# Forget-gate bias of the attention scores: from a DRAM round trip and a masked tile to a second matmul into the same bank

## The reference

```python
def forgetting_attention(q, k, v, logf):
    c = jnp.cumsum(logf, axis=-1)                       # (heads, 256)
    for i in range(S // Q_BLOCK):                       # two blocks of 128 queries
        q0, q1 = i * Q_BLOCK, (i + 1) * Q_BLOCK
        logits = einsum('bhqd,bhkd->bhqk', q[:, :, q0:q1], k[:, :, :q1]) * scale
        logits = logits + (c[:, :, q0:q1, None] - c[:, :, None, :q1])
        logits = jnp.where(causal, logits, -jnp.inf)
        p = jax.nn.softmax(logits, axis=-1)
        outs.append(einsum('bhqk,bhkd->bhqd', p, v[:, :, :q1]))
```

## Time and profile before

| | |
|---|---|
| time, median of 3 runs | 1739.52 us (1736.98 to 1743.05) |
| the profiled execution's own time | 1739.52 us |
| its span, first to last instruction | 1737.6 us |
| mean granted TensorE clock | 0.97 of full speed |
| TensorE busy | 1639.4 us (94%) |
| VectorE busy | 1104.8 us (64%) |
| ScalarE busy | 813.6 us (47%) |
| GpSimd busy | 112.6 us (6%) |

### The profile page before, as it was taken

The page is one execution under the profiler, slowest core; times in us unless marked ns, Lnnn a source line. Parts: engine busy times, 40 slices in busy tenths (PEclk is TensorE's granted clock), DMA queues, the critical chain, the costliest instruction groups (busy, mean ns, idle before and its releaser), DMA issues.

```text
span 1737.6 us, 29051 instructions
## 1 busy us (share of the span) xinstructions
PE 1639.4 (94%) x12246; PEld 1547.7 (89%) x12246; DVE 1104.8 (64%) x1382; ACT 813.6 (47%) x1064; POOL 112.6 (6%) x99
## 2 busy tenths in 40 slices
PE   7999899999999989999888999989999999899998
PEld 6999889998989889999878899978999999799997
DVE  5766768775676668777586566667766544265554
ACT  5454354444534444444586544445444443254442
POOL 1310000000140000000020000001111111000000
PEclk9999999999999999999998999999999999599999
DMA  8856356656676437665432366667765444035552
GB/s 273 274 199 206 110 202 221 232 194 223 217 257 236 141 118 246 215 230 203 157 114 94 114 222 236 241 230 233 252 207 182 146 158 134 25 121 189 182 188 97
DMA packets 232322, 326.62 MB, mean 188 GB/s; under 512 B 7704, under 2 KB 201728, under 8 KB 231680
## 3 DMA queue, kind: packets, MB, share of 16 engines
q1 hardware_dynamic: 222888, 316.16, 54.1%
q10 hardware_dynamic: 9304, 8.59, 1.6%
HBM read 315.28 MB, written 9.45 MB: 187 GB/s over the span
## 4 chain that ended last, share of the span: by engine, by line
PE 75%; issue 8%; DVE 8%; ACT 5%; DMA 2%; POOL 1%; SPq 0%; ACTq 0%; POOLq 0%; DVEq 0%
PE bank L472 23%; PE bank L473 22%; PE bank L474 22%; ACT whi L1019 2%; PE bank L513 2%; DVE wlo L1471 2%; DMA raw<-in_w_in 2%; PE bank L534 1%; POOL rstd L958 1%; PE bank L842 1%; PE bank L670 1%; PE bank L862 1%; PE bank L602 1%; DMA raw<-in_w_ffn_in 1%; PE bank L852 1%
## 5 line engine op out<-in xcount | busy, mean ns | idle before, releaser
L1471 DVE TENSOR_TENSOR wlo<-raw,whi 128x2048 fp32r<-128x2048 f32 (+1 forms) x241 | 548.3, 2277 | 296.6 <-ACT whi L1019 296.3
L1019 ACT ACTIVATE whi<-raw 128x2048 fp32r<-128x2048 f32 (+1 forms) x241 | 456.0, 1894 | 143.0 <-PE bank L474 108.9
L472 PE MATMUL bank<-hT_hi,whi 128*128 128x256 f32 x1728 | 496.9, 288 | 6.6 <-DVE wlo L1471 6.0
L473 PE MATMUL bank<-hT_lo,whi 128*128 128x256 f32 x1728 | 491.3, 284 | 0.0
L474 PE MATMUL bank<-hT_hi,wlo 128*128 128x256 f32 x1728 | 491.2, 284 | 0.0
L472 PEld LDWEIGHTS bank<-hT_hi,whi 128*128 128x128 f32 x1728 | 334.0, 193 | 13.9 <-DVE wlo L1471 6.8
L473 PEld LDWEIGHTS bank<-hT_lo,whi 128*128 128x128 f32 x1728 | 334.2, 193 | 1.2
L474 PEld LDWEIGHTS bank<-hT_hi,wlo 128*128 128x128 f32 x1728 | 333.9, 193 | 0.0
L472 PE MATMUL bank<-whi,hT_hi 128*128 128x256 f32 (+1 forms) x944 | 276.4, 293 | 13.6 <-DVE hT_lo L1534 6.6
L473 PE MATMUL bank<-wlo,hT_hi 128*128 128x256 f32 (+1 forms) x944 | 271.5, 288 | 0.0
L474 PE MATMUL bank<-whi,hT_lo 128*128 128x256 f32 (+1 forms) x944 | 271.3, 287 | 0.0
(11 more groups left out here) (272 smaller groups left out, 1615.3 us busy)
## 6 DMA issues: line engine op xcount, KB each, us to landing
raw<-in_mlp_w SPq DMA_DIRECT2D x64, 1024.0 KB, 5.5
ada_raw<-in_ada_w SPq DMA_DIRECT2D x96, 512.0 KB, 6.4
raw<-in_w_in SPq DMA_DIRECT2D x44, 1024.0 KB, 5.9
raw<-in_w_ffn_in SPq DMA_DIRECT2D x44, 1024.0 KB, 5.2
raw<-in_dil_w_in SPq DMA_DIRECT2D x36, 1024.0 KB, 5.1
raw<-in_w_ffn_out SPq DMA_DIRECT2D x22, 1024.0 KB, 5.0
raw<-in_w_o SPq DMA_DIRECT2D x8, 1024.0 KB, 5.1
bias_near<-near SPq DMA_DIRECT2D x2, 3072.0 KB, 10.3
```

The source lines that it names most:

```text
L472: pe.matmul(dst, lh, rh, start=start, stop=False)
L473: pe.matmul(dst, lh, rl, start=False, stop=False)
L1019: act.activation(view(whi[c % SPL], c), view(raw[c % RAW], c), ACT.Copy).then_inc(s_hi, 1)
L1471: dve.tensor_tensor(view(wlo[c % SPL], c), view(raw[c % RAW], c), view(whi[c % SPL], c).bitcast(F32), ALU.subtract).then_inc(s_lo, 1)
```

## The change

In a score unit each of the two matmuls is followed by a second one into the same columns that accumulates (`start=False`): its stationary operand is column i of the first 8 rows of the identity matrix, spread over 128 columns, and its moving operand is `ncum`, 8 rows. So it adds row i of `ncum` to each of the 128 queries. TensorE waits once for `ncum` ahead of the first unit of a layer. VectorE then reads the mask alone in place of `lbias`; the mask is widened to 384 columns (triangle, zeros, triangle) and is the same for all heads. The store to DRAM, the two spreading DMAs, the waits of SP, and the mask's additions on GpSimd go. `sqh`, `qn` and `mt` get buffers of their own. In layer 0 the angles now stand ahead of `ncum` on VectorE.

```diff
-    c["causal"] = tri
+    c["causal"] = np.concatenate([tri, np.zeros((P, P), np.float32), tri], axis=1)
...
-            lbias = sb("lbias", [P, H1, 3 * P], at=ph)
-            flat = lbias[:, :, :].rearrange("p h k -> p (h k)")
-            sqh = [flat[:, 512 * i:512 * i + 512] for i in range(2)]
-            qn, mt = ([flat[:, a + 512 * i:a + 512 * i + 512].rearrange("p (t n) -> p t n", t=TT) for i in range(2)]
-                      for a in (1024, 2048))
+            sqh = [sb(f"sqh{i}", [P, 512], at=ph) for i in range(2)]
+            qn = [sb(f"qn{i}", [P, TT, 256], at=ph) for i in range(2)]
...
+            mt = [sb(f"mt{i}", [P, 2, S], at=ph) for i in range(2)]
...
+                pe.wait_ge(s_cum, l + 1)
                 g = 0
                 for i in range(H1 + 3):
...
                         for q0, q1, c0 in ((0, P, 0), (P, S, P)):
-                            m = pe.matmul(bk[:, c0:c0 + q1], qT1[r0:r0 + 64, t, q0:q1], kT1[r0:r0 + 64, t, 0:q1],
-                                          start=True, stop=True)
+                            pe.matmul(bk[:, c0:c0 + q1], qT1[r0:r0 + 64, t, q0:q1], kT1[r0:r0 + 64, t, 0:q1],
+                                      start=True, stop=False)
+                            m = pe.matmul(bk[:, c0:c0 + q1], ident[0:H1, i:i + 1].broadcast_to([H1, P]),
+                                          ncum[:, 0:q1], start=False, stop=True)
                         end(m, ("S", u))
...
-                if name[0] == "G" and name[2] == 0:
-                    l = name[1]
-                    sp.wait_ge(s_cum, l + 1)
-                    sp.dma_start(sums_dram[l], ncum[:, :]).then_inc(s_sumsout, 16)
-                    sp.wait_ge(s_sumsout, 16 * (l + 1))
-                    emptied(sp, ("qkT", 4 * l + 3))
-                    for n, k0 in ((1, 0), (2, P)):
-                        sp.dma_start(lbias[:, :, k0:k0 + n * P], sums_dram[l, :, 0:n * P].unsqueeze(0).broadcast_to([P, H1, n * P]))\
-                          .then_inc(s_sumsin, 16)
...
-                pool.wait_ge(s_causal, 16)
-                pool.wait_ge(s_sumsin, 32 * (l + 1))
-                for h in range(H1):
-                    masked = lbias[:, h, :].rearrange("p (s k) -> p s k", k=P)[:, 0:3:2, :]
-                    pool.tensor_tensor(masked, masked, causal[:, :].unsqueeze(1).broadcast_to([P, 2, P]), ALU.add).then_inc(s_lbias, 1)
...
+                if l == 0:
+                    angles()
                 dve.wait_ge(s_zt, l + 1)
                 link(dve.tensor_tensor(mf[:, :], tf[:, :], mf[:, :], ALU.subtract))
                 dve.tensor_tensor_scan(ncum[:, :], mf[:, :], zero1[:, :].broadcast_to([H1, S]), 0.0, ALU.add, ALU.add)\
                    .then_inc(s_cum, 1)
-                if l == 0:
-                    angles()
...
+                dve.wait_ge(s_causal, 16)
...
-                        dve.wait_ge(s_lbias, u + 1)
...
-                            ins = dve.tensor_tensor_reduce(L1[u % 2][:, a:b], bk[:, a:b], lbias[:, i, a:b], 1.0, NEG,
+                            ins = dve.tensor_tensor_reduce(L1[u % 2][:, a:b], bk[:, a:b], causal[:, a:b], 1.0, NEG,
                                                            ALU.add, ALU.max, mx[:, u % 2, t:t + 1])
```

More of the change, by code:

```diff
@@ L105, in block_pair @@
         far_dram = nc.dram_tensor("bias_far", (TT, P, DH, P), F32, kind="Internal").ap()
-        sums_dram = nc.dram_tensor("forget_sums", (DEPTH, H1, S), F32, kind="Internal").ap()
         near_dram = nc.dram_tensor("bias_near", (TT, P, DH, NG * P), F32, kind="Internal").ap()
@@ L117, in block_pair @@
         ident = sb("ident", [P, P])
-        causal = sb("causal", [P, P])
+        causal = sb("causal", [P, 3 * P])
         invcount = sb("invcount", [P, 2, S])
@@ L241, in block_pair @@
         s_fw, s_fwhi, s_fwlo = sem("forget_weights_loaded"), sem("forget_high_ready"), sem("forget_low_ready")
-        s_sumsout, s_sumsin, s_lbias = sem("forget_sums_stored"), sem("forget_sums_spread"), sem("score_bias_ready")
         s_causal, s_inv = sem("causal_loaded"), sem("inverse_counts_loaded")
```

## The result

The changed kernel took 1757.36 us (median of 4 timed runs, 1753.76 to 1760.02), the kernel before 1738.55 beside it (1736.98 to 1743.05). The ratio is 1.0103, with a 95% interval of 1.0075 to 1.0131. So it is slower by 1%. I had forecast 1750.0, with 1738 to 1755 as the range: the sign is right, the size is short by 7.4 us, and the median lies 2.4 us above the range.

The account below looks back on a forecast made before the run. TensorE was taken as the bound, busy 94% of the span. Added columns +10.3, row-count changes +9.6 and the wait gone -9.4 sum to +10.5 us on 1739.52, giving 1750.0 us; range 1738 to 1755.

Parts of the forecast that it names:

- The added columns, +10.3: TensorE, 16 score units: an added 128-column and 256-column matmul each, 0.64 us per unit, 10.3 us in all.
- The change of row count, +9.6: TensorE score units: five changes of row count for two, 0.20 us each, adding 9.6 us over 16 units.
- rivals without drains: Score units: the array does not drain between 64 and 8 rows; +0.9 us, 1740.4 us; chance 18%.
- with units side by side: Score units: added matmuls of the 8 odd units hidden, nothing drains; -4.2 us, 1735.3 us; chance 7%.
- The wait goes, -6.1 of the -9.4: TensorE's gate matmul waits for its low part in both layers' attention: 2.50 and 3.63 us lost, 6.1 in all, vanish.
- The rival that the wait stays in part: Low-part wait: VectorE wins nothing by the convolution, 1.1 us and its slow clock remain in layer 1; 1752.8 us; chance 15%.
- The half-clock echo, -3.3 of the -9.4: TensorE at clock 0.50 behind the low-part waits: 1.65 us lost per layer, 3.3 in all, goes with the waits.

Follow-up runs that it names:

- no bias matmuls: Changed kernel without the 32 added matmuls, so the forget bias is left out of the scores: 1729.94 us, ratio 0.9954.
- before, convolution late: Kernel before, with VectorE's convolution moved from ahead of head 0 to behind the maxima of head 1 and one low part: 1732.53 us, ratio 0.9958.
- split, convolution late: Changed kernel with forget sums split into high and low parts for a one-pass 64-row added matmul, split made earlier, convolution moved behind first maxima: 1735.26 us, ratio 0.9983.
- bias on 64 rows: Changed kernel with the added matmuls run over the 64 rows of their head, 56 of them zero, same columns: 1745.13 us, ratio 1.0032.
- grouped: Changed kernel with both score matmuls of a unit first, then both bias matmuls, same columns: 1744.52 us, ratio 1.0026.
- changed, convolution late: Changed kernel with VectorE's convolution moved behind the first maxima in both layers, units unaltered: 1753.68 us, ratio 1.0091.
- seven changes: Changed kernel with each unit's 256-column score and bias matmuls cut into two of 128 columns, in turns: 1769.49 us, ratio 1.017.
- split bias in its first form: Changed kernel with forget sums split into high and low parts on VectorE, each added matmul a single pass over 64 rows: 1743.28 us, ratio 1.0032.

## Why the prediction was wrong in size

Unit stretches against medians, us, as differences from the kernel before (changes of row count in a unit in brackets):

| kernel | half-clock stretches in them | unit stretches | median |
|---|---|---|---|
| no bias matmuls (2) | 0 | -7.9 | -8.3 |
| before, convolution late (2) | 0 | -8.3 | -7.1 |
| split, convolution late (2) | 0 | -3.7 | -4.4 |
| bias on 64 rows (2) | 0 | +1.5 | +6.9 |
| grouped (3) | 0 | +4.5 | +4.9 |
| changed, convolution late (5) | 2 | +13.5 | +16.1 |
| changed (5), 13 executions, 4 of them profiled | 1 to 3 | +13.5 (+12.0 to +15.0) | +15.0 |
| seven changes (7) | 7 | +27.4 | +29.9 |

Save for the bias on 64 rows, the unit stretches explain the median within 2.6 us. (The split bias in its first form is left out: it lost its time ahead of them.)

*The added columns, +10.3: right.* Bias on 64 rows against no bias matmuls is 184.0 - 174.6 = 9.4 us. But 1.2 us of the 174.6 are what is left of the wait in layer 0, which the longer units cover; without it the columns are 10.6 us, as layer 1 alone says too (92.0 - 86.7 = 5.3 for its half).

*The change of row count, +9.6: right in kind, nearly in size.* The changed kernel at full clock against the bias on 64 rows is 192.6 - 184.0 = 8.6 us for 48 changes, 0.18 each; the other pairs give 0.17 to 0.19, the chain 0.19. The 0.12 that I had read at the 32-row matmul was too low. A change between 64 and 8 rows costs as much as one between 128 and 64. The Trainium skill ("TensorEngine Tiling (Array Packing)", Key Properties) says that a change of mode drains the engine. The traces agree in that every change costs, with this price, if 8 rows count as a mode of their own beside 64; the drain itself no trace shows. The rivals without drains and with units side by side are out: the units, odd and even, are alike at 2.07 us.

*The wait goes, -6.1 of the -9.4: right in size, and in its reasons only by halves.* It is gone in both layers. In layer 1 VectorE did it alone, as the kernel without the bias matmuls shows: the convolution reached 0.5 us a step (1.01 for two at 504.29) and the maxima 0.17. In layer 0 I had VectorE gain 2.5 us, which was 1.42 of the convolution and 1.12 of the maxima of the other layer. The convolution gained nothing, since the pooling sums took the mask's place beside it; VectorE gained 1.4 us elsewhere, and TensorE's own lateness covered the other 1.1. So that the whole wait of layer 0 went is in part luck. The rival that the wait stays in part had this mechanism right, that moved GpSimd work and VectorE slow each other in its new place (11.43 us for an addition of 1.09 in layer 0, 2.10 for a modulation row of 1.28 in layer 1), and its consequence wrong: it left 1.1 us of wait to layer 1, where none is.

*The half-clock echo, -3.3 of the -9.4: this step failed.* I wrote "the wait has an echo" and took it to go with the wait. It did go where nothing else was added: no half-clock stretch is left in the unit stretches without the bias matmuls or with the late convolution. But in the changed kernel the units with five changes put two of them back, at other places, in loops in which TensorE waits for no engine. In the five profiled executions, four of it and one of its form with the late convolution, they were two, three, one, two and two: 3.4 us lost in the mean, as in the one profile of before. So the term is 0, not -3.3. I had priced the changes of row count as time and not as what lowers the granted clock, though I had read from the earlier trace rows that the clock falls behind a pause of TensorE. With this term at 0 the sum is 1739.5 + 13.8 = 1753.3 us, and the median of all 13 executions is 1753.76. That they agree to 0.5 us is in part luck: 1.5 of the +15.0 us stand outside the unit stretches, where my sum has nothing, and its base is 0.8 us above the median of the 64.

*The range.* The other 3.6 us up to 1757.36 are scatter of four runs. The kernel's executions spread over 14.4 us, with a mean clock of 0.960 to 0.971. I summed from one execution to one execution and gave the range no width for that. Why the changed kernel spreads so, while 64 executions of the kernel before stay within 0.965 to 0.972, is not settled. Shown is only, by one pair of profiles 12 us apart, that most of the difference stands outside the unit stretches.

## What to carry to other kernels

Count the changes of the array's row count before adding a thin matmul to a loop: eight rows cost as much as 64, each change costs nearly as much as 128 columns (0.19 against 0.21 us), and five or more in a unit brought the clock down here. Keep the added matmul on the row count of its neighbour, or group them. And before a data path is rebuilt to be rid of a wait, look at what else stands ahead of the late operation in its engine's queue: here moving the convolution gave -7.1 us where rebuilding the path cost 15 to 19. A forecast for a kernel whose clock varies is made for the median of executions, not for the profiled one.

## What the runs showed of the hardware

- A change of row count cost TensorE 0.17 to 0.20 us, between 128 and 64 rows and between 64 and 8 alike; a matmul of 8 rows runs at the pace of 64 (0.21 us for 128 fp32 columns, 0.43 for 256).
- The granted clock can fall to 0.50 for 3.4 us where TensorE waits for no other engine, behind a lengthened unit: both unit stretches together held none of these with two changes (five profiles, without the kernel before and its long waits) and with three (one), one to three with five (five profiles), seven with seven (one).
- One GpSimd addition of 128 x 542 took 11.43 us beside full-size VectorE operations without a pause, and 1.09 beside small ones.
- Thirteen executions of one kernel, not all on the same chip, spread from 1747.07 to 1761.44 us, with mean clocks of 0.971 and 0.960; six of them on one chip from 1749.30 to 1761.44, with 0.969 and 0.960.
